# A two-layer hybrid DiT step on one core: where the key norm's sums, the second half's preparation, the bonus products and two weight splits stand in the engines' orders

## What is computed

```python
q, k, v, u_rwkv, u_fnet = jnp.split(rmsnorm_modulated(x) @ w_in, ...)
# A) windowed attention: one softmax over band keys, context keys and a sink
# B) RWKV-7, two directions:
kk = k * k_k
kk = kk * lax.rsqrt(jnp.sum(kk * kk, axis=-1, keepdims=True) + 1e-12)   # the key norm
a  = sigmoid(a0 + ad @ a_up)                                            # in-context rate
w  = exp(-0.6065 * sigmoid(w0 + tanh(wd) @ w_up))                       # decay
S  = S * w - (S @ kk) (x) (kk * a) + v (x) k_d                           # the scan
bonus = sum(r * k * r_k, axis=-1) * v                                    # added to the scan's y
# C) Fourier mixing of u_fnet over positions and channels
x = x + g1 * (concat(A, B, C) @ w_out); x = x + g2 * ffn(x)
```

## Time and profile before

| | |
|---|---|
| median of 3 runs | 1845.91 us (1845.08 to 1855.27) |
| the profiled execution's own time | 1847.49 us |
| its span, first to last instruction | 1845.5 us |
| granted TensorE clock over the span, 1 is 2.4 GHz | 0.994 |
| preparation of layer 1, fn 0's end to ada_cols(11)'s end | 1073.76 to 1114.53 us |
| the same of layer 0 | 173.30 to 213.97 us |

### The profile page before, as it was taken

How to read it: one execution, slowest core, us unless ns; L and a number is a source line. 1 busy time by engine, 2 the same in 40 slices (tenths; PEclk the granted TensorE clock), 3 DMA queues, 4 the chain that set the end, 5 groups by cost and what they waited for, 6 DMA issues and landing times. The chain is left out here.

```text
span 1845.5 us, 46196 instructions
## 1 busy us (share of the span) xinstructions
PE 1748.4 (95%) x19693; PEld 1634.1 (89%) x19693; DVE 1063.5 (58%) x2328; ACT 800.8 (43%) x1723; POOL 370.5 (20%) x306
## 2 busy tenths in 40 slices
PE   7999988889999999999999998898899999999997
PEld 6999776778899999999989987777798999999997
DVE  4444677663394573838453546676519737465663
ACT  3333555542453351535433346475316525344352
POOL 3254010212302003020324421002232020201112
PEclk9999999999999999999999999999999999999999
DMA  9653600003622313241337254000021232323211
GB/s 338 204 138 110 189 5 3 6 5 107 181 69 81 91 55 107 58 113 53 98 99 200 79 164 92 5 2 7 25 69 47 69 92 81 104 61 89 83 55 58
DMA packets 215973, 161.11 MB, mean 87 GB/s; under 512 B 21968, under 2 KB 213146, under 8 KB 215770
## 3 DMA queue, kind: packets, MB, share of 16 engines
q1 hardware_dynamic: 213818, 156.13, 29.0%
q0 software_dynamic: 1952, 2.03, 0.4%
HBM read 154.99 MB, written 3.15 MB: 86 GB/s over the span
## 5 line engine op out<-in xcount | busy, mean ns | idle before, releaser
L2643 DVE SCALAR_TENSOR_TENSOR x<-PS,mod,x 128x320 f32<-128x320 f32 (+2 forms) x240 | 90.7, 433 | 296.7 <-PE PS L1071 296.7
L1106 PE MATMUL PS<-T_hi,wsplit 128*128 128x320 f32 x768 | 170.0, 309 | 0.0
L811 POOL TENSOR_TENSOR SfR<-ring,SfR 128x768 fp32r<-128x768 f32 (+1 forms) x24 | 41.2, 1715 | 582.2 <-ACT SfR L1768 582.2
L1070 PE MATMUL PS<-in_hi,win 128*128 128x320 f32 x480 | 149.7, 320 | 1.7 <-ACT mix L1836 1.0
L1071 PE MATMUL PS<-in_hi,win 128*128 128x320 f32 x480 | 144.7, 309 | 0.0
L1070 PE MATMUL PS<-hid_hi,wsplit 128*128 128x320 f32 x440 | 133.0, 310 | 0.0
L1071 PE MATMUL PS<-hid_hi,wsplit 128*128 128x320 f32 x440 | 132.5, 309 | 0.0
L1106 PEld LDWEIGHTS PS<-T_hi,wsplit 128*128 128x128 f32 x768 | 128.4, 188 | 0.0
L1106 PE MATMUL PS<-h_hi,wsplit 128*128 128x320 f32 x576 | 127.6, 309 | 0.0
L1106 PE MATMUL PS<-T_lo,wsplit 128*128 128x320 f32 x384 | 118.7, 309 | 0.0
L2079 ACT ACTIVATE wsplit<-Sf 128x512 fp32r<-128x512 f32 x96 | 59.8, 629 | 130.0 <-DVE Sf L2693 72.3
(11 more groups left out here) (536 smaller groups left out, 5413.0 us busy)
## 6 DMA issues: line engine op xcount, KB each, us to landing
ring<-in_w_ada SPq DMA_DIRECT2D x47, 1024.0 KB, 7.9
ring<-in_ffn_w_in SPq DMA_DIRECT2D x88, 512.0 KB, 5.1
ring<-in_ffn_w_out SPq DMA_DIRECT2D x16, 768.0 KB, 4.3
ring<-in_ffn_w_out SPq DMA_DIRECT2D x16, 640.0 KB, 3.9
ring<-in_w_in SPq DMA_DIRECT2D x7, 1024.0 KB, 9.3
ring<-in_w_in SPq DMA_DIRECT2D x10, 512.0 KB, 5.3
ring<-in_w_in SPq DMA_DIRECT2D x16, 256.0 KB, 5.4
ring<-in_w_out SPq DMA_DIRECT2D x16, 256.0 KB, 6.6
```

The costliest lines, as they stand in the source:

```text
L811: nc.gpsimd.tensor_tensor(lo, raw_w, hi, SUB).then_inc(wl_ready(), 1)
L1070: mm(lat[:, 0:TH], w, v[:, 0:TH], start=(n == 0), stop=(n == total - 1))
L1106: last = mm(bank[:, 0:TH], (w_lo if p == 1 else w_hi)[:, k, :], (v_lo if p == 2 else v_hi)[:, k, :], start=(q in (A11, A12, S1_) and k == ...
L2643: last = V.scalar_tensor_tensor(x[:, m, a:b], bank[:, at:at + b - a], mod[:, gate_at + m, s:s + 1], x[:, m, a:b], MUL, ADD)
```

## The change

What it does, for each of the two layers:

- **Key norm.** The kk sums and kinv spreads are no items any more. Both kk sums stand on PE between fn 0 and fn 1, in bank 4; fn 1 is cut into its 8 low-input products, 6 more, then both spreads (into banks 4 to 7), then the last 10. ACT takes squares and roots ahead of the copies of fn 0 and fn 1; DVE inverts and scales inside fn 1's time. A wait of PE for `kk_inv` stands in the middle of fn 1.
- **Half 0.** `prep_exp(0, ...)` goes ahead of fn 0's copy on ACT, as soon as the low products of fn 1 are done; DVE does steps 5, 11, 12 of half 0 right after the key norm. ACT gets two loads of a table ahead of their use (`sigmoid_table`, `exp_table`), in all four switches of table where there were three.
- **Order of PE.** kvT follows fn 1; `ada_rows(8)` stands ahead of the decay products, the other rows between them.
- **Half 1 and bonus.** `prep_exp(1, ...)` stands between the `ft1` copies; DVE's order ahead of attention A is: scans and steps 1 to 4 of half 1; steps 6 to 10 of half 0; steps 5 to 8 of half 1; both bonus products; steps 9 and 10 of half 1. Step 11 stands late in group 0, step 12 late in group 1; attention A and B hold no such step.
- **Scores.** The banks are `ps[2 * g + (m + 1) % 2]`; the first pair waits only for the item ahead of the last.
- **After the scan.** `weight_high(out 2)` comes right after `weight_high(out 1)`, without its wait for out 0; the two gate products stand inside out 1's early rows.

```diff
@@ item_order @@
-    o += [("k", 0), ("v", 0), ("fn", 0), ("kvT", 0), ("fn", 1)]
-    o += [("kk", 0), ("kk", 1)] + lora("w", 1) + lora("a", 0) + lora("a", 1)
-    o += [("kinv", 0), ("kinv", 1), ("ft1", 0), ("ft1", 1), ("ft1", 2)]
+    o += [("k", 0), ("v", 0), ("fn", 0), ("fn", 1), ("kvT", 0)]
+    o += lora("w", 1) + lora("a", 0) + lora("a", 1)
+    o += [("ft1", 0), ("ft1", 1), ("ft1", 2)]
...
@@ tensor engine @@
+                e.wait_ge(kk_sq.sem, kk_sq.upto(l, 2))
+                for t in range(2):
+                    last = quarters(KK_SUM[t], ones64[:, 48:80], 0, 1, rate_sq[t])
+                last.then_inc(kk_ps(), 1)
+
+                fn1 = [(k, 2) for k in range(KT)] + [(k, p) for k in range(KT) for p in range(2)]
+                unit(UNIT_OF[("fn", 1)], fn1[:KT], 3 * KT).then_inc(lo_read(), 1)
+                unit(UNIT_OF[("fn", 1)], fn1[KT:14], 3 * KT, KT)
+                e.wait_ge(swap_read.sem, swap_read.upto(l, 5))
+                e.wait_ge(mrow_sb.sem, mrow_sb.upto(l, 8))
+                e.wait_ge(kk_inv.sem, kk_inv.upto(l, 2))
+                for t in range(2):
+                    spread(*KINV[t], rate_sq[t][:, 0:QW]).then_inc(kinv_ps(), 1)
+                unit(UNIT_OF[("fn", 1)], fn1[14:], 3 * KT, 14)
+
...
-                whole(UNIT_OF[("fn", 1)])
+                e.wait_ge(kinv_taken.sem, kinv_taken.upto(l, 2))
+                ada_rows(8, l)
...
                 lora_rows("w", 1)
...
                 ada_cols(8, l)
                 ada_rows(9, l)
+                lora_rows("a", 0)
+                ada_cols(9, l)
+                lora_rows("a", 1)
+                ada_rows(10, l)
...
                 ft1(1)
-                ada_cols(9, l)
+                ada_cols(10, l)
                 ft1(2)
-                ada_rows(10, l)
...
                     def scores(m):
-                        if m - 2 >= first:
+                        if m - 2 < first:
+                            q_ = (m + 1) % 2
+                            e.wait_ge(acc_free[q_].sem, acc_free[q_].upto(l, (items_before + 1 - q_) // 2))
+                        else:
                             e.wait_ge(s_sb.sem, s_sb.upto(l, 2 * (m - 1)))
...
-                unit(NPROJ + 1, early[n1:], 3 * KT, n1)
-                for t in range(2):
-                    lat, cx = post_begin(("g", t))
...
+                for a, b, t in ((n1, n2, 0), (n2, n3, 1), (n3, len(early), None)):
+                    unit(NPROJ + 1, early[a:b], 3 * KT, a)
+                    if t is not None:
+                        lat, cx = post_begin(("g", t))
...
@@ scalar engine @@
-                e.wait_ge(cum_ready.sem, cum_ready.upto(l, 1))
-                fcopy(0)
...
                 load_root_table()
-                fcopy(1)
+                e.wait_ge(kk_ps.sem, kk_ps.upto(l, 1))
+                for t in range(2):
+                    act(rate_sq[t][:, 0:QW], KK_SUM[t], ACT.Sqrt, bias=eps[:, 1:2]).then_inc(kk_root(), 1)
...
+                e.wait_ge(lo_read.sem, lo_read.upto(l, 1))
+                for part in range(2):
+                    prep_exp(0, part)
+                fcopy(0)
+                act(sigmoid_table[:, :], eps[:, 0:1], ACT.Sigmoid)
+                fcopy(1)
...
+                act(exp_table[:, :], eps[:, 0:1], ACT.Exp)
                 ft1_copy(0)
+                prep_exp(1, 0)
                 ft1_copy(1)
+                prep_exp(1, 1)
                 ft1_copy(2)
...
                 weight_high(NPROJ + 1)
+                weight_high(NPROJ + 2)
...
@@ vector engine @@
                 rate_inverse(0)
                 rate_inverse(1)
+                rate_scale(0)
+                rate_scale(1)
+                e.wait_ge(kinv_taken.sem, kinv_taken.upto(l, 2))
+                for step in (5, 11, 12):
+                    prep(0, step)
                 prep(1, "forward")
                 prep(1, "backward")
...
                 for step in range(1, 5):
                     prep(1, step)
-                for step in range(5, 13):
+                for d in range(2):
+                    taken(e, l, ("a", 0, d))
+                for step in range(6, 11):
                     prep(0, step)
...
+                for step in range(5, 9):
+                    prep(1, step)
+                bonus(0)
+                bonus(1)
+                for step in (9, 10):
+                    prep(1, step)
...
-                attention(0, NATT_A, {4: (bonus, 0), 7: (bonus, 1)})
+                attention(0, NATT_A)
...
                         if g < CTX_GROUP:
-                            prep(1, 8 + 2 * g)
+                            prep(1, 11 + g)
...
-                attention(NATT_A, NATT, {2: (second, 11), 4: (second, 12)})
+                attention(NATT_A, NATT)
```

More of the change, by code:

```diff
@@ L331, in build @@
         rcol = sb("rcol", [128, 5])
-        root_table = sb("root_table", [128, 1])
+        tables_ = sb("root_table", [128, 3])
+        root_table, sigmoid_table, exp_table = (tables_[:, i:i + 1] for i in range(3))
         sink = sb("sink", [128, 8])
@@ L659, in fast_in, with score_bank @@
             return hi[:, k, c], lo[:, k, c], h[:, k, c]
+        KK_SUM = [ps[4][:, 128 + QW * t:128 + QW * t + QW] for t in range(2)]
+        KINV = (ps[4], ps[5][:, 128:256]), (ps[6], ps[7][:, 0:128])
+        def score_bank(m, g):
+            return ps[2 * g + (m + 1) % 2]
         FIRST_INV = ps[5], ps[4][:, 128:256]
@@ L1073, in unit @@
                         last.then_inc(acc_ready(), 1)
+                    return last
                 def first_two(u):
@@ L1763, in weight_high @@
                             e.wait_ge(acc_ready.sem, acc_ready.upto(l, ITEM_AT[("f2", m - 3, part)] + 1))
-                    elif u >= 2 and u != FFN0 + 2:
+                    elif u >= 2 and u not in (NPROJ + 2, FFN0 + 2):
                         e.wait_ge(acc_ready.sem, acc_ready.upto(l, ITEM_AT[UNITS[u - 2][0]] + 1))
@@ L1882, in prep_exp @@
                         act(H[:, 2:4, :], sums, ACT.Exp, scale=-DECAY).then_inc(exps_ready(), 1)
-                for t in range(2):
-                    free, lat, cx = ready(("kk", t))
-                    act(rate_sq[t][:, 0:QW], lat[:, 0:QW], ACT.Sqrt, bias=eps[:, 1:2]).then_inc(free(), 1)
+                e.wait_ge(lo_read.sem, lo_read.upto(l, 1))
[4 more added lines that the diff above has]
+                fcopy(1)
+                free, lat, cx = ready(("kvT", 0))
+                act(vtok[:, 0:NL], lat[:, :], ACT.Copy)
+                act(vtok[:, NL:T], cx[:, 0:128], ACT.Copy)
+                act(kvout[:, :], cx[:, 128:256], ACT.Copy)
+                act(kcT[:, :], cx[:, 256:384], ACT.Copy).then_inc(free(), 1)
+                ada_rows(8, l)
                 lora_sigmoid("w", 1)
+                ada_rows(9, l)
                 lora_sigmoid("a", 0)
                 lora_sigmoid("a", 1)
[L1890 to L1893, removed]
+                ada_rows(10, l)
+                act(exp_table[:, :], eps[:, 0:1], ACT.Exp)
                 ft1_copy(0)
+                prep_exp(1, 0)
                 ft1_copy(1)
+                prep_exp(1, 1)
                 ft1_copy(2)
-                ada_rows(10, l)
                 for t in range(2):
@@ L2395, in _, with attention @@
                 rate_inverse(1)
+                rate_scale(0)
[3 more added lines that the diff above has]
+                    prep(0, step)
                 prep(1, "forward")
                 prep(1, "backward")
[L2398 to L2401, removed]
                 for step in range(1, 5):
                     prep(1, step)
-                for step in range(5, 13):
+                for d in range(2):
+                    taken(e, l, ("a", 0, d))
+                for step in range(6, 11):
                     prep(0, step)
-                def attention(first, last_pair, between):
+                for d in range(2):
+                    taken(e, l, ("a", 1, d))
+                for step in range(5, 9):
[4 more added lines that the diff above has]
+                    prep(1, step)
+                def attention(first, last_pair):
                     def softmax_in(m):
@@ L2447, in attention @@
                             inverse(m - 1)
-                        if m - first in between:
-                            kind, step = between[m - first]
-                            kind(step)
                 e.wait_ge(ld_par.sem, ld_par.upto(l, ld_par.per))
@@ L2458, in _ @@
                 gains(l, 1)
-                def second(step):
-                    prep(1, step)
-                attention(0, NATT_A, {4: (bonus, 0), 7: (bonus, 1)})
+                attention(0, NATT_A)
                 def row_lower(k):
```

50 lines of the change are left out of this document (13 added, 37 removed).

## The result

The changed kernel takes 1839.43 us (median of 13 runs), the kernel before 1847.59 beside it (13 runs): a ratio of 0.995, interval 0.9939 to 0.9961. So it is faster, by 9.2 us (7.2 to 11.3) and not by 18: 1839.4 lies outside the range of 1820 to 1838. The profiled execution took 1841.16 us (span 1839.2), against 1847.5 before.

The account below looks back on a forecast made before the run. PE, busy for 95% of the span, bounds the kernel, so only its idle time can be won. Terms 2.2 + 2.7 + 0.8 + 0.5 + 1.9 + 0.9 make 9.0 us a layer, 18.0 in all: 1828, range 1820 to 1838.

Parts of the forecast that it names:

- preparation ahead of attention A: From fn 0's end to first softmax: PE waits go, a 1.5 us chunk wait comes; attention starts 2.2 us sooner a layer.
- groups 0 and 1: Recurrence rounds: with less DVE work they should last like group 3, 11.35 us on average; 2.7 us a layer.
- attentions A and B: DVE work moved out of both attentions: 0.5 us a layer for A, 0.8 for B.
- behind the scan: After the scan: POOL's low part of out 2 starts sooner, 1.9 us a layer; gate products reach DVE sooner, 0.9.
- Rival 1: Recurrence not paid by DVE: it gives 0.4, the attentions nothing, 5.4 us a layer in all, 1835; chance 0.13.
- the 40.6 forecast: Sign: softmax of layer 1's attention A starts about 40.6 us behind fn 0's end.
- I allow 0.9 for traffic: Ahead of `ada_rows(10)`: 0.9 us added to the second chunk's landing at 22.4, giving a PE wait of 1.5.
- under 2 us: Sign: DVE's wait for line 1882, ACT's second exponentials ahead of attention A, is under 2 us.
- rival 2: DVE late ahead of attention by 2.5 to 4 us: about +1.3 instead of -2.2 a layer, 1835; chance 0.12.
- Rival 4: Key norm not hidden in fn 1: roots late by 3 us cost 2 a layer, 1832; chance 0.05.
- Rival 5: DVE meets POOL between scans and softmax: work stretches by 2.58 / 1.49, 16 us a layer, 1860; chance 0.04.
- Rival 3: Drain at ACT's table switch: exponentials 1.3 us later, softmax 0.9 later a layer, 1830; chance 0.04.

Follow-up runs that it names:

- e4: Changed kernel with three DVE steps of half 1's preparation repeated inside the rounds of groups 0 and 1; 0.9951 of the kernel before.
- e8: Kernel before with three DVE steps of half 1 left out of the rounds, keys of half 1 unscaled; 0.9991 of the kernel before.
- e1: Kernel before with only the two edits behind the scan (ACT's high part of out 2, gate products); 0.9957 of the kernel before, 8.0 us.
- e2: Changed kernel with the two edits behind the scan undone; 0.9987 of the kernel before, 2.4 us.
- e7: Kernel before with only ACT's high part of out 2 ahead of the squares, gate products as before; 0.9966 of the kernel before, 6.3 us.
- e11: Changed kernel run again with no edit; 0.995 of the kernel before.
- e6: Changed kernel with `warm(5)`, five products on constants, ahead of the chunk wait in `ada_rows(10)`; 0.993 of the kernel before.
- e3: Changed kernel with `ada_rows(10)` and `ada_cols(10)` moved behind `ft1(2)`; 0.9924 of the kernel before, 14 us below it.
- e10: Changed kernel with `ada_rows(10)` behind `ft1(2)` and all four rate products ahead of `ada_rows(9)`; 0.9932 of the kernel before.
- e12: Changed kernel with `ada_rows(10)` behind `ft1(2)` and 16 products of 8 columns behind `warm(8)` of layer 0; 0.994 of the kernel before.
- e5: Changed kernel with 64 products of 8 columns added behind `warm(8)` of layer 0; 1.0062 of the kernel before.
- e9: Changed kernel with 16 products of 8 columns added behind `warm(8)` of layer 0; 0.9937 of the kernel before.

## Why the prediction was wrong

The direction was right, and the size was twice too large. By its own terms, in us for both layers:

```text
term                             forecast   measured
preparation ahead of attention A   4.4      -0.9  (43.92 + 42.90 against 42.97 + 42.96)
groups 0 and 1                     5.4       0 to 1.7  (e4, e8)
attentions A and B                 2.6       1.4  (softmax to first square: 0.4, 0.4, 0.2, 0.4 shorter)
behind the scan                    5.6       8.0 (e1), 6.8 (changed kernel against e2)
sum                               18.0       7 to 10; the whole: 9.2
```

**The step that failed first** is the rounds' term: "With DVE then at about group 3's 7.2 us they should last like group 3". DVE came to 7.1 to 7.5 and they lasted 12.3 to 14.7; the work itself is worth 0 to 1.7 us where 5.4 were forecast (e4, e8). I read a correlation of two groups' DVE time with their length as a price, and didn't ask what the gaps themselves said. In the stretches of groups 0 and 1 in the earlier trace rows, in the profile of the kernel before, half of the standing time (1.19 of 2.38 us a group) were block stops, which no engine released; group 3 had 0.1 us of them in layer 0 and 0.3 in layer 1, and that is most of what made it shorter. Rival 1 was this case in outcome, for another reason. Its chance of 0.13 was too low, since nothing in the rows priced the wait that DVE's absence would uncover.

**The second** is the preparation's term. The order was costed well: key norm, scaling and spreads were hidden (no wait on line 960 within fn 1), and with the clock held the stretch lasted 40.1 to 40.4 us against the 40.6 forecast. The chunk wait was 2.2 and 2.3 us and not 1.5, within its bounds of 0 and 2.9; "I allow 0.9 for traffic" was too little. POOL's stores and state loads start at 1085.4 to 1088.1, in the same time; that they made the chunk late isn't shown, and they moved 0.2 of the 3.1 MB between 1084.5 and 1096 us. What had no term and no bound was the clock: seven of the twelve preparations in this order had a fall at the chunk wait, and those stretches were 2.8 us longer (mean 43.0 against 40.2), of which the longer wait is 0.9. DVE's chain is what passed it on: 3.31 us of waiting for the exponentials against "under 2 us". So rival 2, attention late through DVE, is what came to pass there.

Rivals 3 to 5 did not. Rival 4: PE has no wait on line 960 in fn 1's time. Rival 5: DVE's products and sums of two tiles of 128x1280 took 1.49 us there, as in the earlier trace rows. Rival 3, the drain: behind a copy, so with a pipe that had just worked, the switch to the exponentials takes 1.30 us from its start to the next instruction, and no further time stands in front of it. That is half of the 2.66 us that the prediction cites (timeline of ACT, layer 1, after):

```profile
1099.00 0.28 ACT L1797 ACTIVATE mrow<-PS 128x128 f32<-128x128 f32 x1 [3.57 <-PE PS L1040]
1099.29 1.28 ACT L1913 ACT_TABLE_LOAD   x1
1100.59 0.20 ACT L1913 ACTIVATE root_table<-eps 128x1 f32<-128x1 f32 x1
```

One reading was wrong without changing the sum. Beside the slow subtraction of the earlier trace rows, which runs from 1054.14 to 1056.72, POOL did not make a weight's low part, but worked on this product of the key rotation (timeline of POOL, before):

```profile
1053.62 1.74 POOL L854 TENSOR_TENSOR mix<-mix 128x512 f32<-128x512 f32 x1
```

The two overlap for 1.22 us, and the subtraction took 1.09 us longer than with POOL silent, so that it lost about the time of the overlap.

**Behind the scan** the same omission had the opposite sign: the wait for POOL cost its 1.9 us and, in 4 of 6 cases, slow products behind it. e1 and e7 measured 8.0 and 6.3 us where the forecast had 5.6 and 3.8; the intervals of both hold the forecast, so the price of the slow products rests on the traces.

That the wait causes the fall is not shown. Waits of 1.8 us and more came with it 7 times of 7 in that order and shorter ones 0 times of 5, but in e11 it began with the wait and not behind it, and it also fell once over working products (e6) and twice in the old order behind short waits. What e3, e10 and e12 show is that the order without the wait had no fall in six preparations. What that was worth is e3's: 5 us, wait and clock together.

## What to carry to other kernels

Ahead of taking work from an engine because a stretch is long where it is busy, split PE's gaps in that stretch by releaser: gaps without one, at a constant distance in instructions, are its instruction supply. Here they were longer where the other waits were shorter, and work taken off the partner brought 0 to 1.7 us of the 5.4 forecast. A new wait of about 2 us on PE should be priced with the products behind it at the lower clock as the high bound, and a removed one likewise. If a reordering brings a weight chunk nearer to its request, put ready work between them: here ft1's products (4.8 us, free to run once ACT's last sigmoid was done) in between were worth about 5 us.

## What was unexpected of the hardware

- PE waits for instructions: stops of up to 1.92 us in the changed kernel (2.13 in e2) where a block of 256 instructions ends among dense 64x64 products; the shortest distance between two instruction packets in either trace is 3.4 us, about the time in which the rounds use up 256 instructions (some 790 loads and products in 11 to 12 us).
- A product of 4-byte numbers on `ident` and `mats` is four instructions of PE, two loads and two products: 64 of them were 256 numbers in e5, 16 were 64 in e9.
- The 64 products of 8 columns lasted 25 us (32.2 to 57.3), with the lower clock from 35.1 to 62.4 us; the 16 lasted 3.9 us.
